# Inverting the 64-row triangles of a gated delta rule: six doubling steps, or 16-row substitution and two

## The chip, the cores and the metric

One Trainium2 chip, one of its cores. The metric is the device time of one execution in microseconds (us), as the median of several runs. Everything is float32 at the interface. The engines are TensorE (PE, with its weight loads PEld), VectorE (DVE), ScalarE (ACT), GpSimd (POOL) and SyncE (SP), which here does nothing but issue DMAs.

## The reference, cut to what matters

The program computes two transformer blocks over 512 tokens of width 1024. The first has a pooling mixer and a sparse attention. The second has a gated delta rule with four heads beside a banded attention, then a merge, an output projection and a feed-forward part. Only the start of the gated delta rule is touched. Each head's sequence is cut into 8 chunks of 64 tokens, and for each chunk a unit lower triangular 64x64 system is solved:

```python
a_mat = beta[..., :, None] * jnp.einsum('nbhid,nbhjd->nbhij', k, k) * dec_strict
eye = jnp.eye(CHUNK, dtype=jnp.float32)
rhs = jnp.concatenate([(beta * gam)[..., None] * k, beta[..., None] * v], axis=-1)
sol = lax.linalg.triangular_solve(a_mat + eye, rhs, left_side=True, lower=True)
w_c = sol[..., :dk]
uv_c = sol[..., dk:]
...
def step(s, xs):
    w_i, uv_i, p_i, qg_i, kd_i, gl_i = xs
    u = uv_i - jnp.einsum('bhid,bhde->bhie', w_i, s)
    o = jnp.einsum('bhid,bhde->bhie', qg_i, s) + jnp.einsum('bhij,bhje->bhie', p_i, u)
    s = gl_i[..., None, None] * s + jnp.einsum('bhid,bhie->bhde', kd_i, u)
    return s, o
```

With 4 heads and 8 chunks there are 32 such triangles. Both kernels form the inverse of each triangle and multiply by it.

## The kernel before

Every engine has its program written out by hand, and engines meet at named semaphores. There is no scheduler, so the order of the code is the order of each engine's queue.

**Weights and fillers.** All large products are done as three products of split numbers (lines 1457 to 1459: high by high, low by high, high by low). A weight chunk of 128x1024 numbers goes through two slots: SP loads it (`load`, line 519), ACT rounds it to `w_hi` (line 674), POOL or DVE forms `w_lo` (line 498), PE uses it. In stage `fill2` there are 28 such chunks, the projections of the second block that nothing in the delta rule needs. They are cut into 4 pieces each, 112 in all, of 6 matrix products per piece, and PE is given pieces between the steps of the delta rule and of the attention. `FILL2` (line 72) is the table that says how many pieces stand at each place: before, `ready` 3, `first` 4, `level` 18 over 20 places, and 22 over the 16 units of the attention. The same table tells ACT, POOL and DVE at which of their own places they serve the next chunk: ACT and POOL make `w_hi` and `w_lo` of the chunk after next, and DVE copies a finished chunk out of PSUM to `stage2` (line 1007), from where SP stores it (line 523). PE may start chunk n when DVE has copied chunk n-2 (`filled`).

**The triangles.** Loop `h` at lines 1337 to 1368 builds, for each of 4 heads, `a_t` (line 1359): 4 tiles of 128x128, each with two transposed 64x64 triangles on its diagonal. `x_inv` and `y_inv` are to hold the inverse and its transpose. They start as the inverse of the 2x2 diagonal blocks (step `first`, lines 1372 to 1377 on DVE, 1747 to 1753 on PE). Then the block size doubles five times, from 2 to 64: `for k in range(5 * GH)`, five levels by four heads. One such step k is:

- POOL masks the blocks of `a_t` that belong to the level into `b_t` (line 650);
- PE multiplies `x_inv` by `b_t` (line 1778), four products of 128x128;
- ACT copies the result to `bx` (line 933);
- PE forms the corrections (lines 1762 and 1767, four products each), the first only in the first `WITH_X` = 16 steps;
- DVE subtracts them from `x_inv` and `y_inv` (function `update`, line 1379; recorded as line 990, the helper `sub`).

PE's own order is: product k, a piece or none of filler, corrections of k-1. Behind the last step follow the products with the right-hand sides (line 1793) and the recurrence over 8 chunks (lines 1797 to 1821).

## Time and profile before

| | us |
|---|---|
| median of 3 runs | 1685.82 |
| lowest and highest | 1685.09, 1691.6 |
| the profiled execution | 1683.67 |
| its span, first to last instruction | 1681.9 |

The profile tells of one execution. Its page gives busy times per engine, the chain of work that ended last, and groups of instructions by line. The trace behind it can be asked for stretches and lines. A matrix product of float32 by float32 is recorded as two instructions, so that the four products of one line in one step read as x8. Times on the left of a timeline row are us from the start of the span. The word behind an arrow in brackets is what ended an idle time of that engine.

### The profile page before, as it was taken

How to read it: one execution, taken by the hardware profiler on the slowest of the kernel's cores; microseconds unless marked ns; L12 is line 12 of the kernel's file. 1: busy time of each engine (PE TensorE's matmuls, PEld its weight loads, DVE VectorE, ACT ScalarE, POOL GpSimd, SP SyncE). 2: the span in 40 equal slices, each digit the busy share in tenths (PEclk: the TensorE clock that was granted, in tenths of full speed). 3: DMA queues.
4: the chain of work that ended last, by engine and by line, in shares of the span. 5: the costliest groups of instructions: out<-in, count | busy, mean ns of one | idle time of the engine just before them, and what ended most of it. 6: DMA issues, size and time to landing. Idle time of an engine off the chain costs nothing.

```text
span 1681.9 us, 21641 instructions
## 1 busy us (share of the span) xinstructions
PE 1604.2 (95%) x7872; PEld 1275.3 (76%) x7872; DVE 931.2 (55%) x1462; ACT 577.4 (34%) x906; POOL 201.7 (12%) x107
## 2 busy tenths in 40 slices
PE   6997899899999999999999999999899999999997
PEld 4876656688888888887776799676588877787885
DVE  5147466565666665334853832235475778778323
ACT  4231355543333232223325222125444332323221
POOL 3453311100000000000002452132100000000000
PEclk9998999999999999999999999999999999999998
DMA  5421121153233323322332211152253232223231
GB/s 218 160 94 63 57 63 46 58 187 95 93 100 100 98 91 106 102 87 81 98 101 94 75 55 41 38 197 85 77 180 100 88 100 87 90 97 119 86 103 68
DMA packets 49845, 163.10 MB, mean 97 GB/s; under 512 B 5088, under 2 KB 5352, under 8 KB 49648
## 3 DMA queue, kind: packets, MB, share of 16 engines
q1 hardware_dynamic: 46544, 156.09, 27.7%
q10 hardware_dynamic: 3232, 6.08, 1.1%
q8 instruction: 44, 0.72, 0.2%
q14 instruction: 25, 0.20, 0.0%
HBM read 148.50 MB, written 13.65 MB: 96 GB/s over the span
## 4 chain that ended last, share of the span: by engine, by line
PE 83%; DVE 9%; issue 4%; ACT 3%; POOL 0%; DVEq 0%; DMA 0%; ACTq 0%
PE banks L1457 23%; PE banks L1459 23%; PE banks L1458 23%; PE banks L1548 2%; PE banks L1574 2%; PE banks L1557 1%; PE banks L1778 1%; PE banks L1767 1%; PE banks L1631 1%; ACT at_pt L782 1%; PE banks L1762 1%; ACT at_p L773 1%; DVE w_lo L498 1%; PE banks L1820 1%; DVE t_raw L1007 1%
## 5 line engine op out<-in xcount | busy, mean ns | idle before, releaser
L1457 PE MATMUL banks<-h_hi,w_hi 128*128 128x512 f32 x1312 | 532.9, 406 | 33.9 <-POOL w_lo L498 14.4
L1459 PE MATMUL banks<-h_hi,w_lo 128*128 128x512 f32 x1312 | 513.3, 391 | 0.0
L1458 PE MATMUL banks<-h_lo,w_hi 128*128 128x512 f32 x1312 | 512.7, 391 | 0.0
L674 ACT ACTIVATE w_hi<-w_raw 128x1024 fp32r<-128x1024 f32 (+1 forms) x228 | 251.5, 1103 | 447.8 <-PE banks L1459 405.3
L1457 PEld LDWEIGHTS banks<-h_hi,w_hi 128*128 128x128 f32 x1312 | 247.2, 188 | 104.0 <-issue 32.9
L1459 PEld LDWEIGHTS banks<-h_hi,w_lo 128*128 128x128 f32 x1312 | 247.0, 188 | 53.1
L1458 PEld LDWEIGHTS banks<-h_lo,w_hi 128*128 128x128 f32 x1312 | 247.6, 189 | 51.6 <-issue 4.8
L498 DVE TENSOR_TENSOR w_lo<-w_raw,w_hi 128x1024 fp32r<-128x1024 f32 (+1 forms) x167 | 216.7, 1297 | 79.2 <-ACT w_hi L674 79.0
L498 POOL TENSOR_TENSOR w_lo<-w_raw,w_hi 128x1024 fp32r<-128x1024 f32 x61 | 149.0, 2443 | 432.1 <-ACT w_hi L674 432.1
L1457 PE MATMUL banks<-act_hi,w_hi 128*128 128x512 f32 x352 | 137.2, 390 | 1.6 <-DVE t_val L1007 0.8
L1458 PE MATMUL banks<-act_lo,w_hi 128*128 128x512 f32 x352 | 137.0, 389 | 0.0
L1459 PE MATMUL banks<-act_hi,w_lo 128*128 128x512 f32 x352 | 136.9, 389 | 0.0
L773 ACT ACTIVATE at_p<-at_sm,cols 128x128 f32<-128x128 f32 (+3 forms) x96 | 53.2, 555 | 87.0 <-DVE cols L1112 49.5
L1457 PEld LDWEIGHTS banks<-act_hi,w_hi 128*128 128x128 f32 x352 | 66.1, 188 | 16.1 <-DVE t_val L1007 1.2
L1030 DVE TENSOR_TENSOR X<-X,banks 128x512 f32<-128x512 f32 (+1 forms) x32 | 22.0, 688 | 99.6 <-PE banks L1459 99.6
L1459 PEld LDWEIGHTS banks<-act_hi,w_lo 128*128 128x128 f32 x352 | 66.1, 188 | 13.8
L1458 PEld LDWEIGHTS banks<-act_lo,w_hi 128*128 128x128 f32 x352 | 66.1, 188 | 13.6
L742 ACT ACTIVATE act_hi<-t_gate 128x512 f32 (+1 forms) x44 | 27.8, 632 | 132.3 <-DVE t_gate L1093 132.3
L739 ACT ACTIVATE t_gate<-t_gate 128x512 f32<-128x512 f32 x44 | 27.9, 633 | 112.3 <-DVE t_gate L1075 112.3
L636 POOL MEMSET gb_rows<- 64x512 f32 x1 | 0.5, 521 | 545.5 <-DVE w_lo L498 545.5
L1007 DVE TENSOR_TENSOR t_raw<-banks,rms_inv 128x512 f32<-128x512 f32 x66 | 45.5, 689 | 33.9 <-PE banks L1459 27.0
L1574 PEld LDWEIGHTS banks<-at_pt,v_nat 128*64 128x64 f32 x480 | 25.6, 136 | 38.8 <-ACT at_pt L782 30.0
(274 smaller groups left out, 1928.4 us busy)
## 6 DMA issues: line engine op xcount, KB each, us to landing
w_raw<-in_w_up SPq DMA_DIRECT2D x88, 512.0 KB, 3.4
w_raw<-in_w_fill SPq DMA_DIRECT2D x44, 512.0 KB, 3.5
w_raw<-in_w_down SPq DMA_DIRECT2D x32, 704.0 KB, 4.1
late_scratch<-stage SPq DMA_DIRECT2D x44, 256.0 KB, 2.0
w_raw<-in_w_mix SPq DMA_DIRECT2D x16, 512.0 KB, 4.4
sg<-late_scratch SPq DMA_DIRECT2D x16, 512.0 KB, 3.9
w_raw<-in_w_out SPq DMA_DIRECT2D x16, 512.0 KB, 3.5
w_raw<-in_w_in SPq DMA_DIRECT2D x15, 512.0 KB, 3.5
```

The lines of the kernel that those rows point to most:

```text
L498: eng.tensor_tensor(w_lo[:, c.slot, 0:kt * P], w_raw[:, c.slot, 0:kt * P], w_hi[:, c.slot, 0:kt * P], ALU.subtract).then_inc(lo_ready, 1)
L674: act.activation(w_hi[:, c.slot, 0:kt * P], w_raw[:, c.slot, 0:kt * P], ACT.Copy)\
L739: act.activation(t_gate[:, j, :], t_gate[:, j, :], ACT.Silu).then_inc(silu_done[b], 1)
L742: act.activation(act_hi[:, lin(j, 2, i), :], t_gate[:, j, :], ACT.Copy).then_inc(act_hh[b], 1)
L773: act.activation(a.p[:, s % 2, half, 0:w], a.sm[:, half, 0:w], ACT.Exp, bias=a.nbias[:, c:c + 1], scale=DH ** -0.5, accum_out=a.sums[:, c: ...
L1007: return dve.tensor_tensor(dst, src, rms_inv[:, :], ALU.mult)
L1030: dve.tensor_tensor(X[:, m, :], X[:, m, :], bank(ACC + j), ALU.add).then_inc(x_done, 1)
L1457: pe.matmul(dst, w_h, hi[:, kr, :], start=first and n == 0, stop=False)
L1458: pe.matmul(dst, w_h, lo[:, kr, :], start=False, stop=False)
L1459: mm = pe.matmul(dst, w_l, hi[:, kr, :], start=False, stop=last and n == len(ks) - 1)
L1548: return pe.transpose(dst, src, ident[0:n, 0:n])
L1574: mm = pe.matmul(banks[rows(half), BO + j % 2, i * P:(i + 1) * P], v_tile(j, b, half, k), a.pt[:, half, k * P:(k + 1) * P], start=opens an ...
```

## The change

**Blocks of 16 by substitution.** The levels from 2 to 16 are left out. `x_inv` and `y_inv` are zeroed by POOL (two memsets of 128x2048 as soon as the first tile of `in2z` is there). SP stores the four heads of `a_t` to DRAM (`store_a`), and fetches the 16x16 diagonal blocks back with eight DMAs of 16x16x16 (`fetch_blocks`): 128 blocks, one per partition, in `a16`. DVE then inverts all 128 at once in `inv16`: row by row, a product of i x i numbers and a sum over them, 15 rows, each instruction waiting for the one before it (`sub_step`). It also makes the transposed copy. SP stores both (`place_inverses`), waits, and writes them onto the diagonals of `x_inv` and `y_inv` with sixteen DMAs of 16x16x16. PE waits for all sixteen (`inv_in`). Then come two doublings, 8 steps instead of 20, of which the first 4 carry the correction of `x_inv`.

**Fillers.** The 3 + 4 + 18 pieces of the places above become 5 x 4 pieces at a new place `inv`, all of them ahead of PE's first step, and 8 pieces over 8 levels. The units of the attention have 19 instead of 22. `gz` and `gz2` move to other addresses.

The diff, cut to its core:

```diff
-FILL2, FILLED2 = fill_plan([..., ("rows", 4, 2, 1), ("ready", 1, 3, 1), ("first", 4, 1, 1),
-                            ("level", 20, 9, 10), ("chunk", 8, 3, 2), ("out", 4, 3, 1), ("turn", 4, 2, 1),
-                            ("unit", 16, 22, 16)])
+FILL2, FILLED2 = fill_plan([..., ("rows", 4, 2, 1), ("inv", 5, 4, 1),
+                            ("level", 8, 1, 1), ("chunk", 8, 3, 2), ("out", 4, 3, 1), ("turn", 4, 2, 1),
+                            ("unit", 16, 19, 16)])
...
-        WITH_X = 4 * GH
+        WITH_X = GH
+        SUBSTITUTED = 2 * SB + 2
...
+            def store_a(heads):
+                for h in heads:
+                    sp.wait_ge(d_dve, 11 * h + 8)
+                    sp.dma_start(a_dram[:, h * NT:(h + 1) * NT, :], a_t[:, h, :, :]).then_inc(a_stored, 16)
+
+            def fetch_blocks():
+                store_a((2, 3))
+                sp.wait_ge(a_stored, 16 * GH)
+                for n in range(P // SB):
+                    at_ = slice(n * SB, (n + 1) * SB)
+                    sp.dma_start(a16[n * GH * NT:(n + 1) * GH * NT, :, :],
+                                 a_dram[at_, :, at_].rearrange("j n i -> n j i")).then_inc(a16_in, 16)
+
+            def place_inverses():
+                sp.wait_ge(sub_step, SUBSTITUTED)
+                sp.dma_start(inv_dram.rearrange("b n t j i -> (b n) (t j i)"),
+                             inv16.rearrange("p t j i -> p (t j i)")).then_inc(inv_stored, 16)
+                sp.wait_ge(inv_stored, 16)
+                sp.wait_ge(inv_zero, 2)
+                for t, whole_ in ((0, x_inv), (1, y_inv)):
+                    for n in range(P // SB):
+                        at_ = slice(n * SB, (n + 1) * SB)
+                        sp.dma_start(whole_.rearrange("p h c d -> p (h c) d")[at_, :, at_],
+                                     inv_dram[n, :, t, :, :].rearrange("n j i -> j n i")).then_inc(inv_in, 16)
...
-                    late(name, 1, late2, stage2)
+                    late(name, 1, late2, stage2,
+                         {10: lambda: store_a((0, 1)), 11: fetch_blocks, 13: place_inverses})
...
+            def row(i):
+                terms = prod16[:, 0:i * i].rearrange("p (c j) -> p c j", c=i)
+                substituted(dve.tensor_tensor(terms, inv16[:, 0, 0:i, 0:i].rearrange("p j c -> p c j"),
+                                              a16[:, 0:i, i].unsqueeze(1).to_broadcast([P, i, i]), ALU.mult))
+                substituted(dve.tensor_reduce(inv16[:, 0, i, 0:i], terms, AXX, ALU.add))
...
+            for i in range(1, SB):
+                row(i)
+                if i == 9:
+                    serve("inv", 2)
+            substituted(dve.tensor_copy(inv16[:, 1, :, :], inv16[:, 0, :, :].rearrange("p j i -> p i j")))
...
-            fill("ready", 0)
+            for n in range(5):
+                fill("inv", n)
             pe.wait_ge(d_dve, 11 * GH)
-            for h in range(GH):
-                pe.wait_ge(i_mask, h + 1)
-                wait(pe, i_x, h - 1)
-                for p in range(NT):
-                    mm = turn(banks[:, BT + h % 2, p * P:(p + 1) * P], b_t[:, (h + 2) % GH, p, :])
-                mm.then_inc(i_bx, 1)
-                fill("first", h)
-            pe.wait_ge(i_x, GH)
+            pe.wait_ge(inv_in, 16 * 2 * (P // SB))
...
-            for k in range(5 * GH):
+            for k in range(2 * GH):
```

In the order of the built program buffers lose the digits in their names: `inv_131` is `inv16`, `a_132` is `a16`, `prod_133` is `prod16`, `stage_134` and `stage_131` are `stage2`, and `in_w_fill` is the weights of the fillers.

SP's queue in stage `fill2`, around the loads of chunks 10 to 14. Before:

```order
L519 DMA w_raw<-in_w_fill 128x1024 [waits lo_ready]
L523 DMA late_scratch<-stage_131 128x512 [waits filled2]
L519 DMA w_raw<-in_w_fill 128x1024 [waits lo_ready]
L523 DMA late_scratch<-stage_131 128x512 [waits filled2]
L519 DMA w_raw<-in_w_fill 128x1024 [waits lo_ready]
```

After:

```order
L528 DMA w_raw<-in_w_fill 128x1024 [waits lo_ready]
L532 DMA late_scratch<-stage_134 128x512 [waits filled2]
L537 DMA a_scratch<-a_t 128x512 [waits d_dve] x2
L528 DMA w_raw<-in_w_fill 128x1024 [waits lo_ready]
L532 DMA late_scratch<-stage_134 128x512 [waits filled2]
L537 DMA a_scratch<-a_t 128x512 [waits d_dve] x2
L545 DMA a_132<-a_scratch 16x16x16 [waits a_stored]
L545 DMA a_132<-a_scratch 16x16x16 x7
L528 DMA w_raw<-in_w_fill 128x1024 [waits lo_ready]
L532 DMA late_scratch<-stage_134 128x512 [waits filled2]
L528 DMA w_raw<-in_w_fill 128x1024 [waits lo_ready]
L532 DMA late_scratch<-stage_134 128x512 [waits filled2]
```

```order
L551 DMA inv_scratch<-inv_131 128x512 [waits sub_step]
L558 DMA x_inv<-inv_scratch 16x16x16 [waits inv_zero,inv_stored]
L558 DMA x_inv<-inv_scratch 16x16x16 x7
L558 DMA y_inv<-inv_scratch 16x16x16 x8
L528 DMA w_raw<-in_w_fill 128x1024 [waits lo_ready]
L532 DMA late_scratch<-stage_134 128x512 [waits filled2]
```

The second piece follows the first directly. The loads of chunks 11, 12 and 14 now have the stores, the fetches and the placing DMAs of the triangles ahead of them in the one queue.

DVE's queue around the substitution, after the change (its beginning and its end); before, the four pairs of `first` on `y_inv` and `x_inv` stood here:

```order
L1424 MEMSET inv_131 128x256
L1425 MEMSET inv_131 128x16 [waits sub_step]
L1047 TENSOR_TENSOR stage_134<-banks,rms_inv 128x512 [waits late_stored20,chunk_done,sub_step]
L1428 TENSOR_SCALAR a_132<-a_132 128x256 [waits a16_in]
L1420 TENSOR_TENSOR prod_133<-inv_131,a_132 128x1 [waits sub_step]
L1422 TENSOR_REDUCE inv_131<-prod_133 128x1 [waits sub_step]
L1420 TENSOR_TENSOR prod_133<-inv_131,a_132 128x4 [waits sub_step]
```

```order
L1420 TENSOR_TENSOR prod_133<-inv_131,a_132 128x225 [waits sub_step]
L1422 TENSOR_REDUCE inv_131<-prod_133 128x15 [waits sub_step]
L1433 COPY inv_131<-inv_131 128x256 [waits sub_step]
L1047 TENSOR_TENSOR stage_134<-banks,rms_inv 128x512 [waits late_stored20,chunk_done,sub_step]
L1047 TENSOR_TENSOR stage_134<-banks,rms_inv 128x512 [waits late_stored21,chunk_done]
L1047 TENSOR_TENSOR stage_134<-banks,rms_inv 128x512 [waits late_stored20,chunk_done]
```

Between the two pieces stand the other products and sums, and one more copy to `stage_134` behind row 9. The copies of finished filler chunks thus stand inside and behind the substitution.

## Rows read from the trace of the kernel before

**Rows 1.** The page, part 1: busy us, share of the span, instructions.

```profile
PE 1604.2 (95%) x7872; PEld 1275.3 (76%) x7872; DVE 931.2 (55%) x1462; ACT 577.4 (34%) x906; POOL 201.7 (12%) x107
```

**Rows 2.** Busy time in stretches: step `first`, the five levels, the attention.

```profile
core 0: us, PE busy (x) PEld busy (x) DVE busy (x) ACT busy (x) POOL busy (x), PEclk, DMA share, GB/s
957.00:967.00 10.00, 7.76 (x40) 6.03 (x40) 10.00 (x12) 0.28 (x1) 9.88 (x6) 1.00 0.46 156
967.00:1042.80 75.80, 75.03 (x556) 70.39 (x556) 27.73 (x41) 16.61 (x25) 34.12 (x23) 1.00 0.16 53
...
1138.00:1222.00 84.00, 74.39 (x476) 52.01 (x475) 42.00 (x142) 41.99 (x112) 16.25 (x8) 1.00 0.21 71
```

**Rows 3.** Timeline of PE in a level: start, us, line, operation, count.

```profile
1006.30 1.06 PE L1767 MATMUL banks<-y_inv,bx 128*128 128x128 f32 x8
1007.20 1.06 PE L1778 MATMUL banks<-x_inv,b_t 128*128 128x128 f32 x8
1008.01 0.48 PE L1457 MATMUL banks<-h_hi,w_hi 128*128 128x512 f32 x1
...
1009.47 1.05 PE L1762 MATMUL banks<-bx,y_inv 128*128 128x128 f32 x8
```

**Rows 4.** Timeline of PE where `ready` ends and `first` begins.

```profile
955.74 0.39 PE L1459 MATMUL banks<-h_hi,w_lo 128*128 128x512 f32 x1
957.09 0.66 PE L1548 MATMUL banks<-consts,b_t 128*128 128x128 f32 x4 [0.96 <-DVE p2a L1367]
```

**Rows 5.** Timeline of DVE at the end of the last head.

```profile
953.25 1.99 DVE L1359 TENSOR_TENSOR a_t<-dec,beta_strict 128x512 f32<-128x512 f32 x1
955.16 0.68 DVE L1361 TENSOR_TENSOR p2a<-banks,gd_bg 128x512 f32<-128x512 f32 x1
955.76 0.67 DVE L1364 TENSOR_TENSOR k_dec<-banks,gd_kd 128x512 f32<-128x512 f32 x1
...
956.96 0.67 DVE L1007 TENSOR_TENSOR stage<-banks,rms_inv 128x512 f32<-128x512 f32 x1
```

**Rows 6.** Timeline of SP's queue, two DMAs issued back to back.

```profile
957.66 0.34 SPq L523 DMA_DIRECT2D late_scratch<-stage  x1
958.05 0.43 SPq L519 DMA_DIRECT2D w_raw<-in_w_fill  x1
```

**Rows 7.** The page, part 6: DMAs, count, KB each, us from issue to landing.

```profile
w_raw<-in_w_fill SPq DMA_DIRECT2D x44, 512.0 KB, 3.5
late_scratch<-stage SPq DMA_DIRECT2D x44, 256.0 KB, 2.0
...
p2b<-late_scratch ACTq DMA_DIRECT2D x3, 1024.0 KB, 5.6
rel<-rel_scratch ACTq DMA_DIRECT2D x1, 2048.0 KB, 14.0
```

**Rows 8.** Timeline of DVE: a sum, and small instructions that wait for each other.

```profile
1107.87 2.29 DVE L1416 TENSOR_REDUCE o_red<-p2a 128x16 f32<-128x2048 f32 x1 [7.04 <-ACT p2a L949]
...
1207.73 0.16 DVE L1119 RECIPROCAL cols<-cols 128x2 f32<-128x2 f32 x1
1207.93 0.88 DVE L1129 TENSOR_SCALAR at_p<-at_p,cols 128x512 f32<-128x512 f32 x2
```

**Rows 9.** Timelines of DVE and of POOL at the same moment.

```profile
1174.14 2.19 DVE L1112 TENSOR_SCALAR cols<-cols 128x2 f32<-128x2 f32 x1
1173.92 2.39 POOL L498 TENSOR_TENSOR w_lo<-w_raw,w_hi 128x1024 fp32r<-128x1024 f32 x1 [10.50 <-ACT w_hi L674]
```

**Rows 10.** PE behind a long idle time: timeline row, then stretches (PEclk third from last).

```profile
152.82 0.77 PE L1457 MATMUL banks<-h_hi,w_hi 128*128 128x512 f32 x1 [9.12 <-DVE stage L1007]
...
145.00:150.00 5.00, 0.00 (x0) 0.00 (x0) 4.94 (x6) 0.00 (x0) 0.00 (x0) 0.65 0.00 0
150.00:155.00 5.00, 2.18 (x5) 1.82 (x6) 4.83 (x8) 0.00 (x0) 0.00 (x0) 0.50 0.30 84
155.00:157.60 2.60, 2.60 (x15) 1.96 (x14) 2.46 (x6) 0.00 (x0) 0.00 (x0) 0.67 0.39 148
```

More of the change, by code:

```diff
@@ L41 @@
 NCMP = (T - 32) // 16 + 1
+SB = 16
 NEG = -1.0e30
@@ L69, in fill_plan @@
     return plan, total
-FILL2, FILLED2 = fill_plan([("start", 1, 3, 1), ("norm", 8, 2, 1), ("gates", 2, 3, 1), ("rows", 4, 2, 1), ("ready", 1, 3, 1), ("first", 4, 1, 1),
-                            ("level", 20, 9, 10), ("chunk", 8, 3, 2), ("out", 4, 3, 1), ("turn", 4, 2, 1),
-                            ("unit", 16, 22, 16)])
+FILL2, FILLED2 = fill_plan([("start", 1, 3, 1), ("norm", 8, 2, 1), ("gates", 2, 3, 1), ("rows", 4, 2, 1), ("inv", 5, 4, 1),
+                            ("level", 8, 1, 1), ("chunk", 8, 3, 2), ("out", 4, 3, 1), ("turn", 4, 2, 1),
+                            ("unit", 16, 19, 16)])
 FILL1, FILLED1 = fill_plan([("start", 1, 3, 1), ("norm", 6, 2, 1), ("turn", 3, 2, 1), ("compress", 5, 1, 1), ("scores", 2, 4, 1),
@@ L633, in _, with mask @@
             serve()
+            pool.wait_ge(copied["in2z"], 1)
+            pool.memset(x_inv[:, :, :, :], 0.0).then_inc(inv_zero, 1)
+            pool.memset(y_inv[:, :, :, :], 0.0).then_inc(inv_zero, 1)
             pool.wait_ge(copied["in2z"], 5)
+            pool.memset(gb_rows[:, :], 0.0).then_inc(blk_zero, 1)
             pool.wait_ge(lo_ready, BASE["fill2"] + 2)
-            pool.memset(gb_rows[:, :], 0.0).then_inc(blk_zero, 1)
             serve = lows("fill2", FILL2, FILLED2)
+            def mask(k):
+                pool.tensor_tensor(b_t[:, k % GH, :, :], a_t[:, k % GH, :, :], level(4 + k // GH), ALU.mult)\
+                    .then_inc(i_mask, 1)
             for h in range(GH):
-                if h < 3:
-                    serve("rows", h + 1)
-                if h == 2:
-                    serve("ready", 0)
-                pool.wait_ge(d_dve, 11 * (h + 1) if h < 2 else 11 * GH)
-                pool.tensor_tensor(b_t[:, (h + 2) % GH, :, :], a_t[:, h, :, :], level(0), ALU.mult).then_inc(i_mask, 1)
-            for k in range(5 * GH):
-                pool.wait_ge(i_bx, k + 1)
-                pool.wait_ge(i_y, min(k + 1, GH))
-                pool.tensor_tensor(b_t[:, (k + 2) % GH, :, :], a_t[:, k % GH, :, :], level(1 + k // GH), ALU.mult)\
-                    .then_inc(i_mask, 1)
-                serve("first", k) if k < GH else serve("level", k - GH)
-            for k in range(4 * GH, 5 * GH):
+                serve("rows", h)
+            for n in range(5):
+                serve("inv", n)
+                if n < GH:
+                    pool.wait_ge(d_dve, 11 * GH)
+                    mask(n)
+            for k in range(2 * GH):
+                if k < GH:
+                    pool.wait_ge(i_bx, k + 1)
+                    mask(GH + k)
                 serve("level", k)
@@ L925, in _ @@
                 serve("rows", h)
-            serve("ready", 0)
-            for h in range(GH):
-                serve("first", h)
-            for k in range(5 * GH):
-                act.wait_ge(i_bx, GH + k + 1)
+            for n in range(5):
+                serve("inv", n)
+            for k in range(2 * GH):
+                act.wait_ge(i_bx, k + 1)
                 wait(act, i_pe, corrected(k - 2) if k >= 2 else 0)
@@ L1368, in _, with substituted @@
                     .then_inc(d_dve, 1)
-            serve("ready", 0)
-            dve.wait_ge(d_dve, 11 * GH)
-            for h in range(GH):
-                dve.wait_ge(i_mask, h + 1)
-                sub(y_inv[:, h, :, :], every(ident), b_t[:, (h + 2) % GH, :, :]).then_inc(i_y, 1)
-                dve.wait_ge(i_bx, h + 1)
-                sub(x_inv[:, h, :, :], every(ident), bank(BT + h % 2, NT)).then_inc(i_x, 1)
-                serve("first", h)
+            serve("inv", 0)
+            sub_steps = [0]
+            def substituted(ins):
+                sub_steps[0] += 1
+                ins.then_inc(sub_step, 1)
+                dve.wait_ge(sub_step, sub_steps[0])
+            def row(i):
[3 more added lines that the diff above has]
+                substituted(dve.tensor_reduce(inv16[:, 0, i, 0:i], terms, AXX, ALU.add))
+            substituted(dve.memset(inv16[:, 0, :, :], 0.0))
+            substituted(dve.memset(inv16[:, 0, :, :].rearrange("p j i -> p (j i)")[:, 0:SB * SB:SB + 1], 1.0))
+            serve("inv", 1)
+            dve.wait_ge(a16_in, 16 * (P // SB))
+            substituted(dve.tensor_scalar(a16[:, :, :], a16[:, :, :], -1.0, None, ALU.mult))
+            for i in range(1, SB):
[3 more added lines that the diff above has]
+            substituted(dve.tensor_copy(inv16[:, 1, :, :], inv16[:, 0, :, :].rearrange("p j i -> p i j")))
+            assert sub_steps[0] == SUBSTITUTED
+            for n in (3, 4):
+                serve("inv", n)
             def update(k):
```

39 lines of the change are left out of this document (24 added, 15 removed).

## The prediction, made before the changed kernel ran

> **What bounds the kernel now.** I read the engines' shares first: PE is busy 1604.2 of 1681.9 us, no other engine over 55% apart from PE's own weight loads [rows 1]. So what PE does there sets the time unless a wait opens. Then I read the stretches of the touched stage: step `first` takes 10.0 us with PE busy 7.76, the five levels 75.8 us with PE busy 75.03 [rows 2]. The levels are full of PE work, and no chain of waits shows through. The reader is to see two things. Matrix products taken out of the levels come off the time one for one. And whatever the change puts in their place must end no later than PE runs out of filler.
>
> **What PE loses.** A group of four products of 128x128 takes 0.90 us (1006.30 to 1007.20); a group and a piece of filler 2.27 us (1007.20 to 1009.47), so a piece is 1.37 us [rows 3]. Before, the levels have 20 + 16 + 20 = 56 groups and 18 pieces: 50.4 + 24.7 = 75.1, against 75.8 measured. After: 8 + 4 + 8 = 20 groups and 8 pieces, 18.0 + 11.0 = 29.0, and the same 0.7 of edges: 29.7 us. The groups give back 32.4 us. `first` gives back its 10.0 us less four pieces of 5.5 us, so 4.5 [rows 2]. Pieces in this stage go from 25 to 28, which adds 4.1 us here and takes 4.1 us off the attention.
>
> **When PE could start the levels.** Pieces of `inv` begin where those of `ready` did. Three end at 956 [rows 4]; the fourth opens chunk 9, for which DVE must have copied chunk 7, which it does at 956.96 to 957.6 [rows 5]. 17 pieces from 957.7 give 981.0. If nothing else were late, the levels would end at 981.0 + 29.7 = 1010.7 instead of 1042.8. That is 32.1 us earlier, and 36.2 with the attention's share. This is the floor.
>
> **The new chain.** It is what I expect to be last, so I follow it from the last `a_t`, ready at about 955.2 [rows 5].
> - *Store of `a_t`.* SP stands in its order: the store of chunk 7 (957.66), the two stores of heads 0 and 1, the load of chunk 11, the store of chunk 8, then heads 2 and 3. The store of chunk 8 waits for DVE's copy behind the two small memsets, at about 958.8. Back-to-back issues are 0.39 us apart [rows 6]. So the last store is issued at 960, and lands 2.0 us later like other stores of 256 KB [rows 7], a little more beside a load of 512 KB: 962.7.
> - *Eight fetches.* No row has a DMA with pieces as short as 64 bytes (16x16 of them). Lower bound: only its issue, 0.4 us [rows 6]. Upper bound: by the piece, from the copy of 1 MB in pieces of 2 KB. That is 512 pieces, 32 for each of 16 DMA engines, in 5.6 less 2.0 us: 0.11 us a piece, 1.8 us for 16 of them [rows 7]. Loads with pieces of 4 KB take (3.5 - 2.0) / 8 = 0.19 us a piece [rows 7]. A straight line through both leaves 0.03 us for a piece without length, 0.5 us a DMA. I take 0.5 since it is near the issue row too. The DMA of 2 MB in 14.0 us gives the same 0.19 for pieces of 2 KB and shares its time with loads, so it is not used. Eight are 4.0 us, and the last lands 2.0 later: 968.7.
> - *Substitution.* 32 dependent instructions (a negation, 30 of the rows, a copy). Small ones follow each other at 0.20 us (1207.73 to 1207.93), a sum over 2048 numbers takes 2.29 us, 0.16 and 1.04 ns a number [rows 8]. The rows have twice 1240 numbers, negation and copy 512 at most at that rate: 32 x 0.20 + 2992 x 0.00104 = 9.5 us. The copy of chunk 9 inside adds 0.6. POOL adds more: an instruction on 128x2 numbers took 2.19 us while POOL's 2.39 us product ran [rows 9], and the last `a_t` took 1.99 instead of 0.68 [rows 5]. POOL has two masks and one or two `w_lo` in this time; from 0 to 5 us, I take 2.5. End: 968.7 + 12.6 = 981.3.
> - *Placing.* SP must first issue the store of chunk 10, which DVE copies behind the substitution: 0.7 + 0.4. Store of `inv16` 2.0, sixteen placements 16 x 0.5 = 8.0, landing 2.0. PE is let go at 994.4.
>
> A rule of the Trainium skill speaks against these DMAs. Its page "DMA: Bandwidth & Descriptors", section Specifications, says that below 512 bytes a DMA engine reads, modifies and writes instead of only writing; no row here has such pieces to show it. It comes back among the rivals.
>
> **PE meanwhile.** The stall inside the fillers costs nothing at the end. Chunk 11 needs the copy of chunk 9, which DVE makes behind row 9 (about 974), while PE is there at 968.7; chunk 12 needs the copy of chunk 10, at 982. Five pieces are left then, 6.9 us, so PE has done its fillers by 989 and idles some 5 us. Its clock falls in such idle times: after 9.12 us of idling the granted clock was 0.50 of full speed in 150 to 155 and 0.67 up to 157.6 [rows 10], so it ran at 1.2 instead of 2.4 GHz for about 4 us from 152.8. That costs 2 us on the levels. Fully idle or half-speed, the fillers still end ahead of 994.
>
> The page "SBUF — State Buffer", section "SBUF: two separate sides", explains the slow DVE instructions: a shared port that one engine holds for a whole instruction. By that rule each of four POOL operations could hold the substitution once; the trace agrees in kind, a stall of 2.0 us under one product [rows 9].
>
> **Sum.** Levels end at 994.4 + 2 + 29.7 = 1026.1 instead of 1042.8: 16.7 us. The attention has 74.39 of 84 us of PE work, so three pieces less uncover some idling [rows 2]: of 4.1 us I count 2.5, between 1 and 4.1. Together 19.2. The chunk 14 loads behind the placements on SP's queue at about 992.9, lands at 997, is rounded and split by 1001; PE wants it in the fourth level, at about 994.4 + 2 + 11: hidden. POOL's zeroing of 2 x 2048 columns comes a stage earlier, behind work of PE. The masks, copies and updates that go from POOL, ACT and DVE save nothing, since PE is busy through 75.03 of the levels' 75.80 us [rows 2]. The profiled execution of 1683.67 would be 1664.5; the median lies 2.15 us above it: **1666.5 us**.
>
> **Rivals.**
> - *PE is the bound.* DMAs at 0.4 us (24 x 0.1 = 2.4 us less), no hold by POOL (2.5 less) and landings 0.5 us shorter (four of them, 2.0 less) end the chain at 987.5, 6.5 us behind the floor; without the lower clock that leaves 32.1 - 6.5 = 25.6 and up to 4.1 of the attention, 29.7 us: 1656. At the floor itself 36 us, 1650. For it: every step has slack in its rows. Against it: it needs all of them at the short end.
> - *Short pieces cost twice.* Each of the 24 DMAs takes about 1.0 us instead of 0.5: 12 us longer, a gain of 7, 1679. By rows this lies between 0.4 and 1.8. What the skill's rule on pieces under 512 bytes would do is this.
> - *The fillers run dry.* ACT waits in its order for the load of chunk 14 ahead of the copy `bx` of step 1, and POOL for ACT ahead of its masks. If that load is late by some 6 us behind the placements, PE waits for `bx`: 1672.
> - *Slower than before.* By the piece, at 1.8 us a DMA: 24 x 1.3 = 31 us, and the gain of 19 becomes a loss of 12, 1698. It decides from 0.5 + 19.2 / 24 = 1.3 us a DMA. For it: SP issues all of them in one queue and none is hidden by PE work after 989. Against it: it takes the whole cost as one per piece, whatever its length, and the two rows differ with length.
> - *It doesn't do what it says.* Were the fetched triangles not needed so early, no wait would open; but PE's first level reads `x_inv`, so the wait is real. I give it nothing.
>
> **How the numbers follow.** Forecast 0.45, PE as the bound 0.17, short pieces twice 0.17, fillers dry 0.13, slower 0.08. Range 1652 to 1682: it takes in the forecast with its own bounds (DMA 0.4 to 0.7 us, POOL 0 to 5 us, attention 1 to 4.1), the dry fillers, most of the first two rivals, and leaves out the slower case and the floor. 0.5%, about what a measurement of this kernel can tell from no change, is 8.4 us: faster means under 1677.4. That is the forecast, the first and the third rival and a good third of the second: 0.81. Same: 0.12; slower: 0.07.
>
> **What would show it.** In the new profile: 20 pieces of filler in a row on PE, an idle time of about 5 us ended by a DMA, half the clock for some 4 us behind it, and the levels in about 30 us. On SP's queue the eight fetches should be issued 0.4 to 0.5 us apart and the sixteen placements too; distances of 1 us and more there point to the second or fourth rival. On DVE the 15 rows should take 10 to 13 us, with single instructions over 1 us beside POOL's. I am wrong if PE never waits for `inv_in`, or if the placing DMAs take over 20 us.

## The result and the profile after

The changed kernel takes 1679.22 us as the median of 7 runs (1675.61 to 1683.47), beside 1688.4 us of the kernel before (7 runs, 1685.09 to 1691.6). The ratio is 0.9947, with a 95% interval from 0.9929 to 0.9965: 9 us less, where the forecast had 19.3. The two profiled executions differ by 8.06 us: 1675.61 (span 1673.8) and 1683.67.

The page after, parts 1, 2 and 5, answers to [rows 1]. PE is busy 25.1 us less, but the span is only 8.1 us shorter, so 17 us of new idling have opened. The tenths of the granted clock show an 8 in two slices. The one in the fourth slice was there before [rows 10]; the one in the 24th, at 962 to 1004 us, is new. It lies where PE waits for the new chain.

```profile
span 1673.8 us, 20961 instructions
...
PE 1579.1 (94%) x7568; PEld 1247.4 (75%) x7568; DVE 917.0 (55%) x1464; ACT 571.0 (34%) x894; POOL 182.6 (11%) x93
...
PEclk9998999999999999999999989999999999999999
...
L1516 PE MATMUL banks<-h_hi,w_hi 128*128 128x512 f32 x1312 | 535.4, 408 | 51.3 <-DVE stage L1047 27.0
```

The last row is the first of the three products of split numbers: PE idled 51.3 us ahead of its 1312 instances, 27.0 of it until DVE had copied a chunk of fillers out (`stage`). That is the row to follow.

The same stretches as [rows 2], by windows of the trace after (stretch, its length, then busy us and count of PE, PEld, DVE, ACT, POOL, the granted clock, DMA share, GB/s): from `ready` to the first level, the two levels, then two pieces of place `out`, then the attention.

```profile
957.00:997.44 40.44, 25.94 (x104) 20.40 (x103) 16.27 (x43) 4.23 (x4) 14.61 (x8) 0.87 0.39 109
997.44:1029.31 31.87, 30.79 (x209) 28.38 (x209) 9.37 (x14) 7.74 (x11) 12.22 (x7) 0.95 0.26 90
1097.00:1104.00 7.00, 3.28 (x8) 2.66 (x9) 3.58 (x3) 1.38 (x3) 4.18 (x2) 0.70 0.77 250
1104.00:1111.00 7.00, 5.39 (x24) 4.08 (x22) 1.97 (x3) 0.63 (x1) 0.00 (x0) 0.81 0.34 133
1138.00:1206.00 68.00, 59.58 (x408) 40.03 (x408) 38.18 (x132) 36.54 (x104) 11.97 (x5) 1.00 0.19 67
```

The levels fell from 75.8 to 31.9 us, but PE stands idle or at half its clock in much of the 40 us ahead of them. SP's queue in that stretch, as a timeline, shows the new chain (issue, us of the issues, line, what, count):

```profile
959.31 0.94 SPq L537 DMA_DIRECT2D a_scratch<-a_t  x2
960.29 0.46 SPq L528 DMA_DIRECT2D w_raw<-in_w_fill  x1
960.79 0.46 SPq L532 DMA_DIRECT2D late_scratch<-stage  x1
961.29 0.98 SPq L537 DMA_DIRECT2D a_scratch<-a_t  x2
967.32 3.94 SPq L545 DMA_DIRECT2D a<-a_scratch  x8
...
986.05 0.43 SPq L551 DMA_DIRECT2D inv_scratch<-inv  x1
988.31 3.76 SPq L558 DMA_DIRECT2D x_inv<-inv_scratch  x8
992.11 3.88 SPq L558 DMA_DIRECT2D y_inv<-inv_scratch  x8
```

The eight fetches take 0.49 us each, the sixteen placements 0.48. DVE between them:

```profile
972.59 0.29 DVE L1428 TENSOR_SCALAR a<-a 128x256 f32<-128x256 f32 x1 [12.54 <-DMA a<-a_scratch]
972.91 0.16 DVE L1420 TENSOR_TENSOR prod<-inv,a 128x1 f32<-128x1 f32 x1
973.11 0.15 DVE L1422 TENSOR_REDUCE inv<-prod 128x1 f32<-128x1 f32 x1
...
976.52 2.07 DVE L1420 TENSOR_TENSOR prod<-inv,a 128x81 f32<-128x81 f32 x1
978.63 0.24 DVE L1422 TENSOR_REDUCE inv<-prod 128x9 f32<-128x81 f32 x1
...
984.53 0.39 DVE L1433 COPY inv<-inv 128x256 f32<-128x256 f32 x1
```

12.3 us in all, 0.20 us apart at first, and one product of 81 numbers took 2.07 us. On POOL the `w_lo` of a chunk ran then:

```profile
976.04 2.40 POOL L507 TENSOR_TENSOR w_lo<-w_raw,w_hi 128x1024 fp32r<-128x1024 f32 x1 [5.94 <-ACT w_hi L715]
```

And PE's waits, from its timeline. The first three rows are the stall in the fillers, the start of the levels and their end (the first product with a right-hand side). The next two are in place `out`, the last is the first product of the attention:

```profile
979.74 0.76 PE L1516 MATMUL banks<-h_hi,w_hi 128*128 128x512 f32 x1 [9.54 <-DVE stage L1047]
...
997.44 2.05 PE L1831 MATMUL banks<-x_inv,b_t 128*128 128x128 f32 x8 [3.32 <-issue]
...
1029.31 1.16 PE L1846 MATMUL banks<-y_inv,p2a 128*128 128x128 f32 x8 [1.08 <-DVE y_inv L1030]
...
1100.72 0.77 PE L1516 MATMUL banks<-h_hi,w_hi 128*128 128x512 f32 x1 [4.69 <-DVE stage L1047]
...
1120.74 0.50 PE L1516 MATMUL banks<-h_hi,w_hi 128*128 128x512 f32 x1 [2.06 <-POOL w_lo L507]
...
1135.88 0.49 PE L1616 MATMUL banks<-p2b 64*128 64x128 f32 x4 [0.69 <-ACT v_nat L1015]
```

In the kernel before the same marks are:

```profile
1042.83 0.94 PE L1793 MATMUL banks<-y_inv,p2a 128*128 128x128 f32 x6 [0.78 <-DVE y_inv L990]
...
1139.33 0.49 PE L1557 MATMUL banks<-p2b 64*128 64x128 f32 x4 [0.69 <-ACT v_nat L975]
```

So the levels end 13.5 us earlier, and the attention begins only 3.45 us earlier. Ten of the microseconds gained are lost between the two, in code that the diff doesn't touch.

**Stages.** The stretch ahead of `ready` differs by up to 3 us between executions of kernels that are alike there, here by 1.26. So I cut the time at marks: the start of the last product of `ready`'s third piece (955.74 before [rows 4], 957.00 after), the levels' end, the first product of the attention, and the merge behind it (1214.03 and 1206.08). Stage A is then from `ready` to the levels' end, B the recurrence with `out` and `turn`, and C the attention. All profiles together, in us, are read off like rows shown here:

| kernel | A | B | C | sum, less before | ratio of medians |
|---|---|---|---|---|---|
| before | 87.1 | 96.5 | 74.7 | | |
| after | 72.3 | 106.6 | 70.2 | -9.2 | 0.9947 |
| e10 after, again | 72.3 | 106.5 | 70.2 | -9.3 | 0.9946 |
| e1 copy early | 74.7 | 100.8 | 70.2 | -12.6 | 0.9928 |
| e2 old phase | 77.4 | 96.5 | 74.7 | -9.7 | 0.9917 |
| e3 before, shifted | 91.2 | 105.9 | 72.0 | +10.8 | 1.0055 |
| e4 no chain | 55.4 | 106.5 | 70.2 | -26.2 | 0.9846 |
| e5 shift by four | 76.2 | 96.4 | 69.9 | -15.8 | 0.9880 |
| e11 the same, again | 72.4 | 96.5 | 70.0 | -19.4 | 0.9886 |
| e9 stores alone | 65.7 | 106.5 | 70.2 | -15.9 | 0.9913 |
| e6 stores and shift by four | 65.7 | 96.5 | 69.9 | -26.2 | 0.9832 |
| e12 the same, again | 64.6 | 98.1 | 70.0 | -25.6 | 0.9847 |
| e7 two queues | 64.1 | 96.5 | 71.3 | -26.4 | 0.9833 |
| e8 copies ahead | 65.5 | 96.5 | 70.0 | -26.3 | 0.9836 |

### The profile page after: what moved, and what is told of

Same layout as the page of the kernel before. It is cut to its first block, busy times and chain, and to the rows that moved or that the text cites. A ratio compares the mean times of both kernels' runs of the same rounds, so it can differ in the third digit from the quotient of the medians.

```text
span 1673.8 us, 20961 instructions
## 1 busy us (share of the span) xinstructions
PE 1579.1 (94%) x7568; PEld 1247.4 (75%) x7568; DVE 917.0 (55%) x1464; ACT 571.0 (34%) x894; POOL 182.6 (11%) x93
## 4 chain that ended last, share of the span: by engine, by line
PE 80%; DVE 9%; issue 4%; ACT 3%; DMA 1%; POOL 1%; DVEq 0%; SPq 0%; ACTq 0%
PE banks L1516 23%; PE banks L1518 23%; PE banks L1517 23%; PE banks L1607 2%; PE banks L1633 2%; PE banks L1616 1%; PE banks L1690 1%; ACT at_p L814 1%; ACT at_pt L823 1%; DVE w_lo L507 1%; PE banks L1873 1%; DVE t_raw L1047 1%; PE banks L1872 1%; DVE at_sm L1148 1%; DVE cmp_blk L1247 1%
## 5 line engine op out<-in xcount | busy, mean ns | idle before, releaser
L1516 PE MATMUL banks<-h_hi,w_hi 128*128 128x512 f32 x1312 | 535.4, 408 | 51.3 <-DVE stage L1047 27.0
L1633 PEld LDWEIGHTS banks<-at_pt,v_nat 128*64 128x64 f32 x480 | 25.6, 136 | 37.7 <-ACT at_pt L823 30.0
```

Source lines behind the costliest of these rows:

```text
L1516: pe.matmul(dst, w_h, hi[:, kr, :], start=first and n == 0, stop=False)
L1633: mm = pe.matmul(banks[rows(half), BO + j % 2, i * P:(i + 1) * P], v_tile(j, b, half, k), a.pt[:, half, k * P:(k + 1) * P], start=opens an ...
```

## Experiments

### Whose loss is `out`

**Theory (shift).** The change moves every place behind the levels by three pieces: 61 pieces stand ahead of the recurrence where there were 58, so `out` begins at piece 73 and no longer at 70. Chunk n opens at piece 4n, and needs DVE's copy of chunk n-2. DVE makes that copy at the first of its places by which the chunk's pieces are complete. Before, the piece that opens chunk 19, number 76, stood in the third turn of `out`, and the copy of chunk 17 a turn earlier. Now piece 76 stands in the second turn, and the copy of 17 at DVE's `serve("out", 0)`. In both kernels that copy is the first instruction behind the norm in DVE's queue. What moved is PE's need for it: PE takes the first two turns of `out` ahead of its transposes, which wait for the norm, and the third behind them. Before, DVE's copy and PE's first product of chunk 19 were

```profile
1113.32 0.68 DVE L1007 TENSOR_TENSOR stage<-banks,rms_inv 128x512 f32<-128x512 f32 x1
1117.42 0.47 PE L1457 MATMUL banks<-h_hi,w_hi 128*128 128x512 f32 x1
```

so the copy was done 3.4 us ahead. DVE's timeline after:

```profile
1094.32 2.29 DVE L1475 TENSOR_REDUCE o_red<-p2a 128x16 f32<-128x2048 f32 x1 [7.76 <-ACT p2a L989]
1097.56 2.29 DVE L1478 TENSOR_TENSOR p2a<-p2a,o_red 128x2048 f32<-128x2048 f32 x1 [0.95 <-ACT o_red L999]
1099.88 1.29 DVE L1047 TENSOR_TENSOR stage<-banks,rms_inv 128x512 f32<-128x512 f32 x2
```

Its first copy is done at about 1100.6, when PE starts; PE had come to piece 76 at about 1096. **Rival (late memory work).** The loss comes from the new memory traffic of the chain or from the moved memsets and addresses, not from the plan of fillers.

*e3: the kernel before, with the levels given the three pieces.*

```diff
-                            ("level", 20, 9, 10), ("chunk", 8, 3, 2), ("out", 4, 3, 1), ("turn", 4, 2, 1),
-                            ("unit", 16, 22, 16)])
+                            ("level", 20, 21, 20), ("chunk", 8, 3, 2), ("out", 4, 3, 1), ("turn", 4, 2, 1),
+                            ("unit", 16, 19, 16)])
```

> The kernel before with nothing changed but the filler table: 21 instead of 18 pieces over the levels and 19 instead of 22 over the attention's units, the same shift by 3 pieces that the change brings. Theory A: the stall in `out` appears here too, 8 to 10 us slower than before, ratio 1.005 to 1.006. Theory B: within 1 us of before, ratio 1.000.

Measured: 1697.29 us, ratio 1.0055 [1.0039, 1.0071]. Its PE timeline has the same two waits, to 0.02 us, without any substitution in the program:

```profile
1120.82 0.77 PE L1457 MATMUL banks<-h_hi,w_hi 128*128 128x512 f32 x1 [4.69 <-DVE stage L1007]
...
1140.12 0.50 PE L1457 MATMUL banks<-h_hi,w_hi 128*128 128x512 f32 x1 [2.04 <-POOL w_lo L498]
```

The shift alone makes the kernel before slower by about 9 us. A grew by 4.1 us (three pieces), B by 9.4, and C gave back 2.7. The rival falls. (C gave back less here than the 4.5 of the changed kernel: PE's clock was half for 3.4 us in it, from about 1186.8 to 1190.2, which costs 1.7.)

*e2: the changed kernel, with `out` where it was.* `inv` gets 17 pieces instead of 20, the units 22.

```diff
-                            ("rows", 4, 2, 1), ("inv", 5, 4, 1),
+                            ("rows", 4, 2, 1), ("inv", 5, 17, 5),
...
-                            ("unit", 16, 19, 16)])
+                            ("unit", 16, 22, 16)])
```

> The changed kernel with 17 instead of 20 pieces at place `inv` and 22 instead of 19 over the attention's units, so that places `chunk` and `out` stand at the same pieces as before the change. Theory A: no stall in `out`; PE starts the levels when the DMAs let it, as now, so the 3 pieces cost their 4 us in the attention and gain nothing ahead of the levels: 1679 - 10 + 4 = 1673, ratio 0.991. Theory B: 1679 + 4 = 1683, ratio 0.997.

Measured: 1673.77 us, ratio 0.9917 [0.9887, 0.9946]. The median is the 1673 expected, but the profiled execution has one term more. B is 96.5 us again, as before. The attention gave nothing now (74.7), and A is 5.1 us longer: in this run the store of `inv16` took 5.7 us to land instead of 2.3, and the half clock behind it lasted 6.8 us instead of 3.4. So three pieces less in `inv` shorten nothing, since the chain sets the start of the levels.

*e1: the plan as changed, DVE's copy ahead of the norm.*

```diff
                 if c == NCH - 1:
                     serve("chunk", c)
+                    serve("out", 0)
                     break
```

> The changed kernel with one edit: DVE copies finished filler chunk 17 right behind the last step of the recurrence instead of behind the norm of its output. Theory A (the shift of the filler table by 3 pieces moves the opening of chunk 19 into place `out` 1, where its copy of chunk 17 has not been made; PE idles 4.7 us there, its clock falls, and the next chunk is late too): the stall of 4.7 us and the half clock behind it go, 7 to 10 us less than the changed kernel's 1679, so 1669 to 1672, ratio to before 0.989 to 0.991. Theory B (the missing gain went into the new chain of DMAs and substitution alone): within 2 us of 1679, ratio 0.994.

Measured: 1674.7 us, ratio 0.9928 [0.9903, 0.9953]. The wait for DVE is gone, but POOL's `w_lo` is next in line, 1.68 us in its place, and 2.05 later:

```profile
1100.39 0.50 PE L1517 MATMUL banks<-h_hi,w_hi 128*128 128x512 f32 x1 [1.68 <-POOL w_lo L507]
...
1117.68 0.50 PE L1517 MATMUL banks<-h_hi,w_hi 128*128 128x512 f32 x1 [2.05 <-POOL w_lo L507]
```

B fell from 106.6 to 100.8 us: 5.8 of the 10, less than the 7 to 10 expected. PE idled 3.0 us less, and the other 2.8 came from the clock, which stayed full. The wait for DVE with its half clock was the larger part, the rest belongs to the others served by the same table.

*e5: shifted by a whole chunk, four pieces.* `inv` 21, units 18: then the chunks fall to the places as before, one chunk on.

```diff
-                            ("rows", 4, 2, 1), ("inv", 5, 4, 1),
+                            ("rows", 4, 2, 1), ("inv", 5, 21, 5),
...
-                            ("unit", 16, 19, 16)])
+                            ("unit", 16, 18, 16)])
```

> The changed kernel with the filler table alone edited: 21 pieces at place `inv` and 18 over the attention, a shift by 4 pieces (one whole chunk) against the kernel before, where the change shifts by 3. Theory A (what costs in `out` is where chunk boundaries fall): both stalls in `out` vanish (4.7 us and 2.1 us and the half clock), the one more piece hides in front of the levels: 1668 to 1671, ratio 0.989. Theory C (any later start of the table costs, since the copies come late): like the changed kernel, 1679.

Measured: 1669.63 us, ratio 0.988 [0.9843, 0.9918]. No wait for a copy or a `w_lo` in `out`, B 96.4 us, and C 69.9. A was 76.2 in this run, again with a late landing of `inv16`'s store (4.1 us); in e11, the same kernel, it was 72.4.

### What the chain costs

*e4: no chain.* Nothing is stored, fetched, substituted or placed; PE waits only for the zeroing of `x_inv`. The inversion of the 16x16 blocks is left out, and the levels work on zeros.

```diff
-            for i in range(1, SB):
-                row(i)
-                if i == 9:
-                    serve("inv", 2)
+            serve("inv", 2)
...
-                         {10: lambda: store_a((0, 1)), 11: fetch_blocks, 13: place_inverses})
+                         {})
...
-            pe.wait_ge(inv_in, 16 * 2 * (P // SB))
+            pe.wait_ge(inv_zero, 2)
```

> The changed kernel with the whole chain left out: no store of a_t, no fetches, no substitution on DVE, no placing DMAs; x_inv and y_inv stay zero, and PE waits only for their memsets. It shows what the chain costs as PE sees it. If the chain sets the start of the levels (forecast: at 994 against a floor of 981, and 2 us of lower clock): 14 to 17 us less than the changed kernel, 1662 to 1665, ratio 0.984 to 0.986. If PE were the bound already: 1679, ratio 0.994.

Measured: 1660.86 us, ratio 0.9846 [0.9817, 0.9876]. This is the floor of PE's own work: A is 55.4 us, 31.7 less than before, where the prediction's floor had 32.1. So the chain costs 72.3 - 55.4 = 16.9 us of PE's time. `out` lost its 10 us here too.

```profile
1012.98 0.49 PE L1823 MATMUL banks<-y_inv,p2a 128*128 128x128 f32 x2 [1.08 <-DVE y_inv L1030]
```

*e6: the stores of `a_t` earlier.* In the changed kernel the four stores share the DMA engines with chunk 11's load and chunk 8's store, and two of them stand behind these in the queue. Two waits of SP's own queue in this stretch, after (us in all, count, longest):

```profile
SPq L545 <- DMA a_scratch<-a_t: 5.0, 1, 5.0
SPq L558 <- DMA inv_scratch<-inv: 1.7, 1, 1.7
```

e6 is e5 with all four issued at chunk 10's load, each as soon as its head is ready, and with fetches and placements ahead of the store of a chunk.

```diff
             def fetch_blocks():
-                store_a((2, 3))
...
-                if c >= 3:
-                    store_late(b, scratch, stage, c - 3)
...
+                    if c >= 3:
+                        store_late(b, scratch, stage, c - 3)
...
-                         {10: lambda: store_a((0, 1)), 11: fetch_blocks, 13: place_inverses})
+                         {10: lambda: store_a(range(GH)), 11: fetch_blocks, 13: place_inverses})
```

> The kernel e5 with SP's queue reordered: all four stores of a_t ahead of the store of chunk 7 and of the load of chunk 11, the fetches and the placing DMAs each ahead of the store of a finished chunk. Theory: the last store of a_t took 5 us to land beside other transfers and stood behind two stores and a load; it now lands at about 960 instead of 967, and placing starts 1 us earlier after the substitution. PE's first level starts 6 to 8 us earlier: 1662 to 1664. Rival (the landing is a fixed cost of a store to DRAM): 2 to 3 us, 1667.

Measured: 1659.3 us, ratio 0.9832 [0.9802, 0.9861], 29 us less than before, and under the 1662 to 1664 expected. Beside e5 that is 10 us, but e5 had the late store. Beside e11, the same kernel as e5, A is 6.7 us shorter (65.7 and 72.4), which lies in the 6 to 8 expected. SP's and PE's timelines:

```profile
946.59 8.61 SPq L537 DMA_DIRECT2D a_scratch<-a_t  x4
957.27 0.34 SPq L532 DMA_DIRECT2D late_scratch<-stage  x1
957.65 0.43 SPq L528 DMA_DIRECT2D w_raw<-in_w_fill  x1
958.14 4.10 SPq L544 DMA_DIRECT2D a<-a_scratch  x8
...
979.78 0.32 SPq L550 DMA_DIRECT2D inv_scratch<-inv  x1
981.76 3.75 SPq L557 DMA_DIRECT2D x_inv<-inv_scratch  x8
985.56 3.88 SPq L557 DMA_DIRECT2D y_inv<-inv_scratch  x8
...
991.03 1.13 PE L1830 MATMUL banks<-x_inv,b_t 128*128 128x128 f32 x8 [0.57 <-issue]
```

The fetches begin at 958.14 instead of 967.32; counted from `ready` that is 7.5 us sooner. DVE starts 7.2 us sooner, counted from `ready` (963.71 and 972.59, from 955.35 and 957.00). PE is let go 4.8 us sooner, with hardly a wait (0.57 us), so its clock doesn't fall and the levels take 30.0 us instead of 31.9. What lies between went to POOL: it was busy in a larger part of the substitution, whose rows took 16.1 us up to the next store, not 13.5. Four of DVE's products were held, here three of them:

```profile
964.42 2.35 DVE L1419 TENSOR_TENSOR prod<-inv,a 128x4 f32<-128x4 f32 x1
...
966.99 1.03 DVE L1419 TENSOR_TENSOR prod<-inv,a 128x9 f32<-128x9 f32 x1
...
970.13 2.11 DVE L1419 TENSOR_TENSOR prod<-inv,a 128x64 f32<-128x64 f32 x1
```

*e7: half the small DMAs on ACT's queue.* e6, with four fetches and the eight placements of `y_inv` issued by ACT.

```diff
+            act.wait_ge(inv_stored, 16)
+            act.wait_ge(inv_zero, 2)
+            for m in range(P // SB):
+                at_ = slice(m * SB, (m + 1) * SB)
+                act.dma_start(y_inv.rearrange("p h c d -> p (h c) d")[at_, :, at_],
+                              inv_dram[m, :, 1, :, :].rearrange("n j i -> j n i")).then_inc(inv_in, 16)
```

> The kernel e6 with half of the eight fetches and half of the sixteen placing DMAs issued by ACT. Theory (these DMAs cost their issue, 0.48 us each, and nothing by piece): 4 x 0.48 + 8 x 0.48 = 5.8 us off the chain; PE's fillers end at 985 to 990, so that 4 to 6 us come off: 1658. Rival (the DMA engines' work on short pieces is the limit, or one descriptor generator serves both queues): no gain.

Measured: 1660.72 us, ratio 0.9833 [0.9807, 0.9859], no gain. The sixteen placements were issued in 5.2 us on the two queues (980.77 to 985.97), beside 7.7 on one, so the queues do work side by side. The last placement is issued 3.6 us sooner, but at e6 PE's fillers and the chain already end together, and what A gains (64.1) C loses (71.3). That loss is the clock's: in C it was half for 6.8 us (about 1129.2 to 1136.0), in e6 for 3.4, which makes some 1.4 us. Why it fell for longer is not known. *e8* adds that DVE copies chunks 9 and 10 ahead, before the fetched blocks and in row 9:

```diff
+            serve("inv", 2)
             dve.wait_ge(a16_in, 16 * (P // SB))
...
-                    serve("inv", 2)
+                    serve("inv", 3)
```

> The kernel e7 with DVE's copies of finished chunks moved ahead: chunk 9's in front of the substitution and chunk 10's behind row 9. Theory: PE no longer idles some 9 us within its fillers, which only matters if they end behind the chain; the fillers then end near 985, and PE's clock falls once instead of twice: 0 to 4 us less than e7, 1655 to 1658. Rival (the chain still ends last by far): as e7.

Measured: 1659.45 us, ratio 0.9836 [0.9803, 0.9869]. The stalls in the fillers fall from 1.65 and 4.94 us (e7) to 1.64, 0.79 and 2.03, and nothing follows: PE has less to do at the end of the chain, and waits there (4.07 us) instead. But the chain itself also ended later: the store of `inv16` was issued at 981.95 instead of 978.80. SP, no longer held by the store of the copy of chunk 9, issued the next load at 967.03 instead of 973.87. So a `w_lo` of POOL ran at 975.48, in the middle of the substitution, where in e7 it ran at 983.05, behind it, and one more product of DVE was slow beside it (2.19 us for 144 numbers). So e8 doesn't isolate the stall: the earlier copies set POOL going sooner, in DVE's way. That a stall in the fillers is hidden as long as the chain ends later is read from the wait behind them.

### Do the two edits add up

Four kernels on one chip: the changed one, with the stores' order alone, with the shift alone, with both.

> The changed kernel as it is, for a square of four kernels on one chip: as it is, with the order on SP's queue changed, with the filler plan changed, with both. Expected: ratio to the kernel before 0.9947, as measured first, some 9 us. In the profile: the stall of 4.7 us in place out ended by DVE's copy, the first level at about 996 to 998.

> The changed kernel with its own filler plan, but SP issues the four stores of a_t together at the load of chunk 10, ahead of the store of chunk 7, and fetches and placements go ahead of the store of a chunk. Theory that two separate terms were mis-sized (the landing of a_t's stores and the place out): the chain ends 8 to 10 us earlier, the levels too, the stall in out stays; ratio 0.988 to 0.990, between the kernel as it is and the one with both edits, and the two edits add up: about 10 us for this one, 8 to 10 for the filler plan. Rival, that the earlier chain only uncovers the PE bound and gains little without the filler plan: 3 us or less, ratio 0.993 or more. Second rival, that the gain of both edits together was the order on SP's queue alone and the filler plan gives nothing: ratio 0.983, equal to the kernel with both.

> The changed kernel with 21 pieces in place inv and 18 in the units, no other edit. Expected as measured before: ratio 0.988, no stall in out. This is the third corner of the square.

> Both edits: 21 pieces in place inv, and the stores of a_t issued together early. Expected as measured before: ratio 0.983, levels start at about 991, no stall in out. If the two edits add up, its distance to the unchanged one is the sum of the two single ones, within 3 us.

| kernel | median, us | less after | ratio to before (1686.43) |
|---|---|---|---|
| e10 after | 1678.34 | | 0.9946 [0.9928, 0.9965] |
| e9 stores alone | 1671.58 | 6.8 | 0.9913 [0.9879, 0.9947] |
| e11 shift alone | 1665.31 | 13.0 | 0.9886 [0.9852, 0.9919] |
| e12 both | 1659.31 | 19.0 | 0.9847 [0.9814, 0.9881] |

6.8 + 13.0 = 19.8 beside 19.0: they add up, within the scatter of medians of four to ten runs that spread over 5 to 8 us. By the marks of the profiles, e9 shortens A by 6.6 us and nothing else, and e11 shortens B by 10.1, while A and C stay within 0.2. That A stays is a balance: its levels began 2.1 us later behind the late store of `inv16`, and took 2.0 us less at full clock. So the two losses are separate, as far as this scatter tells. Neither rival of e9 holds: A alone gave 6.6 us, where the first had 3 at most, and e9 and e12 differ by 9.8 us at the marks, where the second had nothing. But e9 gave less than the 10 us expected, and its interval takes in 0.993. PE's waits in e9 show the same stall in `out` as after:

```profile
993.97 1.13 PE L1830 MATMUL banks<-x_inv,b_t 128*128 128x128 f32 x8 [1.74 <-issue]
...
1095.57 0.76 PE L1515 MATMUL banks<-h_hi,w_hi 128*128 128x512 f32 x1 [4.69 <-DVE stage L1046]
```

e11's median gained 13.0 us, its profile 10.1. I expected 8 to 10 for this edit. The 3 us between lie within the scatter of the medians, and I have no cause for them.

## Why the prediction was right and wrong

The direction was right, and the size was twice what came: 19.2 us forecast, 8.06 measured between the two profiled executions. The difference of 11.1 us, term by term:

| term | forecast | measured | adds |
|---|---|---|---|
| ahead of `ready` | 0 | +1.26 | 1.3 |
| levels end (A) | -16.7 | -14.8 | 1.9 |
| `chunk`, `out`, `turn` (B) | 0 | +10.1 | 10.1 |
| attention (C) | -2.5 | -4.5 | -2.0 |
| behind it | 0 | -0.1 | -0.1 |

**The step that failed** is in "What PE loses": "Pieces in this stage go from 25 to 28, which adds 4.1 us here and takes 4.1 us off the attention." It priced the three pieces by their work alone. But the table of fillers also says which chunk PE opens at which place, and so which copy, rounding and `w_lo` must be ready there. DVE's copy of chunk 17 stands behind the norm, two instructions of 2.29 us, in both kernels. Moved by three quarters of a chunk, PE wanted it in the second turn of `out`, ahead of its transposes, and no longer in the third, behind them. It stood for 4.69 us, and POOL's `w_lo` held it 2.06 more. In the first wait its clock fell to half, and stayed there up to about 1106.7 (0.70 and 0.81 of full speed in the two windows of 7 us shown above). Stretch B before and after, as windows:

```profile
1042.83:1139.33 96.50, 93.33 (x520) 69.94 (x520) 28.59 (x54) 26.71 (x34) 20.04 (x8) 1.00 0.33 115
1029.31:1135.88 106.57, 96.65 (x520) 71.95 (x520) 27.39 (x53) 25.88 (x33) 18.14 (x8) 0.97 0.31 109
```

The same 520 products took 3.3 us longer, since some 5.9 us of them ran at the half clock (3.0 of the 3.3, as an estimate), and PE idled 9.9 us instead of 3.2, 6.7 more, which are the two waits. Together they are the 10.1. The prediction never followed the table past the levels. A count of the pieces at `out`, 73 and not 70, beside the place of the norm in DVE's queue, would have shown it. That it needs no substitution, e3 showed, and e2, e5 and e11 that it goes when the shift is undone or made a whole chunk.

**The chain** came out close, step by step, when each is counted from `ready` (1.26 us taken off after's times):
- *Stores of `a_t`.* Mis-sized: the last was issued at about 960.5, as forecast 960, but SP went on only at 966.1, not 962.7. It took 5.0 us of waiting. The four stores, 1 MB in all, shared the DMA engines with 512 KB of weights and two stores of 256 KB, all issued between 958.9 and 962.3. I had added 0.7 us for the load. e6 and e9 removed this wait, and A became 6.6 us shorter in e9. Both also put fetches and placements ahead of a store; what each of the two moves gave was not separated.
- *Fetches.* 0.49 us each against 0.5; the last landed sooner than 2.0 us behind its issue. DVE began at 971.3, forecast 968.7: 0.8 of the 3.4 us came back here.
- *Substitution.* 12.3 us against 12.6. The 0.20 us from one small instruction to the next was exact, and the product slow beside POOL took 2.07 us, which else takes about 0.3 (its neighbours with 64 and 100 numbers 0.27 and 0.40), where I had 2.5 for all holds together.
- *Placing.* 0.48 us each against 0.5, and 1.45 us from the last issue to PE instead of 2.0. The store of `inv16` landed after 2.3.
- *PE let go* at 996.2, forecast 994.4. The wait behind the fillers was 3.3 us, forecast some 5, and the granted clock was 0.95 over the levels' 31.87 us, which cost 1.6, forecast 2. The profile names no DMA for that wait ("issue"), but it ends 1.45 us behind the last placement.
- *The levels* in 31.9 us, less 1.6 for the clock: 30.3, forecast 29.7. And the floor, 31.7 us by e4, forecast 32.1.

The stall inside the fillers (9.54 us, ended by DVE's copy) costs nothing here, as the prediction said: PE still waits 3.32 us behind its fillers, and in e2, with a stall of 15.21 us, it waits 5.26. No run removed the stall alone; e8 shortened it, and lengthened the chain. Chunk 14's load was hidden, as forecast: no wait for it shows in PE's rows.

**The attention** gave more than I counted, 4.5 us and not 2.5: three pieces less were three pieces' time and a little more. That they lay wholly on the path was the upper end of my bound, 4.1: PE's busy time in C fell by 4.07 us (65.77 to 61.70).

**The rivals.** "Short pieces cost twice" foretold 1679, and the median is 1679.22. But it is the wrong reason: it would have needed 1.0 us for each of the small DMAs, and the rows give 0.48 and 0.49. The Trainium skill's rule that I set beside it ("DMA: Bandwidth & Descriptors", Specifications: below 512 bytes a DMA engine reads, modifies and writes) is not to be seen in these rows: with pieces of 64 bytes the issue alone sets the rate. Whether the engines do more behind the issue no run shows, since landings of 1.8 to 1.9 us left nothing to find. "The fillers run dry" didn't happen. "Slower" needed 1.3 us a DMA. None of my rivals had the loss that came, in a place the diff leaves alone; the range of 1652 to 1682 held the time only since others reached there.

The Trainium skill's page "SBUF — State Buffer", section "SBUF: two separate sides", has one engine holding a port for a whole instruction. The trace agrees: in e6 a product over 4 numbers took 2.35 us beside POOL's 2.40 and ended with it (966.77 and 966.75), while in the changed kernel the sum at 978.63, which reads one operand, took its 0.24 us within a mask of POOL that ran from 978.40 to 979.72.

## What to carry to other kernels

A table that spreads filler work is a schedule for every engine that serves it. Whoever moves work from one place of it to another has moved each later need and each later service too; shift by whole chunks, or count anew, up to the end of the table, where PE now needs each copy, rounding and load and where these stand in their engines' queues. A chain of small DMAs was bound by its issues here (0.48 us each) and by what else is in flight when its large part is stored; issue that part as soon as each piece of it is ready. And an agreement in the total says nothing of the cause: read it stage by stage.

The version with both edits, e6 (and again e12), beats both kernels: 0.9832 [0.9802, 0.9861] and 0.9847 [0.9814, 0.9881] of the kernel before, 19 us less than the changed one.

## What the hardware showed that I had not expected

- *A wait of PE of 3 to 5 us can cost some 3 us more by the clock, but need not.* After 3.32 us of idling ahead of the levels, the products of the changed kernel ran at 1.2 instead of 2.4 GHz for 3.4 us (997.44 to 1000.9: a product of 128x512 took 0.63 us, later 0.39), and likewise in e10 after 3.35. In `out` the stretch was 6.8 us, in e3 as well. It began within the wait of 4.69 us, at about 1099.8 in the changed kernel and at about 1118.4 in e3, so that 5.9 and 4.4 us of products ran in it, and B lost 10.1 and 9.4 us. But e1 had 6.8 us after 3.82, e5 6.8 after 3.19, and e11 none after 3.76. After 0.57 us (e6) and 1.74 us (e9) the clock stayed full. In e12 the clock fell to 0.76 in 1097 to 1104 with no wait over 1.39 us just ahead, which is the 1.6 us that its B is longer. What decides between them stays open.
- *A store of 256 KB lands between 2.0 and 5.7 us.* That of `inv16` took 2.0 us in e6, e9 and e12, 2.3 in after, e10 and e1, but 4.0 in e11 and 4.1 in e5, with the same order on SP's queue as in after, and 5.7 in e2, right behind a load of 512 KB. For e2 the load is a reason; for e5 and e11 I have none, and it stays open.
- *DMAs with pieces of 64 bytes cost no more than their issue*, 0.48 us, whether they read DRAM into `a16` or write onto the diagonals of `x_inv`; with two queues (e7) eight took 4.62 us on SP's, 0.58 each, and eight 3.98 on ACT's at once.
- *Small instructions of DVE can be slower by ten times beside POOL*: 2.35 us for a product of 128x4 numbers with both operands in SBUF, where else 0.17. The sums, with one operand, weren't slow in these rows.
